# Level products for the later halves, one predicated copy a half, and two modulation steps a part: a decoder kernel of two blocks on Trainium2

## The reference

```python
b = jnp.cumsum(gt, axis=2)                      # gt: log of the forget gate
diff = b[:, :, :, None, :] - b[:, :, None, :, :]
decay = jnp.exp(jnp.where(causal, diff, -jnp.inf))
attn = jnp.einsum('bhtd,bhsd,bhtsd->bhts', qt, kt, decay)
o = einsum('bhts,bhsv->bhtv', attn, vt) + einsum('bhtd,bhdv->bhtv', qt * exp(b), state)
state = exp(b_last) * state + einsum('bhsd,bhsv->bhdv', kt * exp(b_last - b), vt)
```

## Time and profile before

| | |
|---|---|
| runs | 2058.63 us median of 3 (2056.67 to 2058.8) |
| profiled execution | 2055.89 us, span of its instructions 2054.0 us |
| PE busy | 1671.7 us (81%) |
| DVE busy | 1047.3 us (51%) |
| POOL busy | 668.8 us (33%) |
| ACT busy | 550.0 us (27%) |
| DMA | 309 GB/s mean over the span |
| mean granted TensorE clock | 0.924 |

### The profile page before, as it was taken

The page is one execution under the profiler, slowest core; times in us unless marked ns, Lnnn a source line. Parts: engine busy times, 40 slices in busy tenths (PEclk is TensorE's granted clock), DMA queues, the critical chain, the costliest instruction groups (busy, mean ns, idle before and its releaser), DMA issues.

```text
span 2054.0 us, 21828 instructions
## 1 busy us (share of the span) xinstructions
PE 1671.7 (81%) x8580; PEld 1024.8 (50%) x8580; DVE 1047.3 (51%) x1910; ACT 550.0 (27%) x948; POOL 668.8 (33%) x413
## 2 busy tenths in 40 slices
PE   6979887787777777787999988999998877677766
PEld 5866852232232223236989868987894221121211
DVE  6955576876778675453664897554434100000001
ACT  4422431122212212124453435445621000000001
POOL 4422553444444444423664555433320000000000
PEclk9999898999999999998999999999998877777777
DMA  8655499999999999974545323544585999999997
GB/s 328 237 200 225 153 376 422 421 421 421 422 422 420 409 422 421 418 328 146 185 144 174 125 102 104 200 164 148 189 349 202 408 421 421 422 421 421 422 421 305
DMA packets 92212, 634.73 MB, mean 309 GB/s; under 512 B 10924, under 2 KB 13612, under 8 KB 16456
## 3 DMA queue, kind: packets, MB, share of 16 engines
q1 hardware_dynamic: 50400, 351.82, 43.7%
q0 software_dynamic: 36864, 268.45, 31.7%
q10 hardware_dynamic: 4840, 13.00, 1.8%
HBM read 632.15 MB, written 1.08 MB: 308 GB/s over the span
## 4 chain that ended last, share of the span: by engine, by line
DMA 40%; PE 36%; DVE 16%; issue 4%; ACT 3%; POOL 0%; ACTq 0%; DVEq 0%; SPq 0%; POOLq 0%
DMA t<-in_expert_uv,t 19%; DMA t<-in_eg 5%; DMA t<-in_ed 5%; DMA ring<-in_ed 5%; PE ps L538 4%; PE ps L540 4%; PE ps L542 4%; PE ps L709 3%; DVE t L1927 3%; PE ps L710 3%; PE ps L585 3%; DVE t L1721 3%; DMA ring<-in_eg 3%; PE ps L572 2%; PE ps L557 2%
## 5 line engine op out<-in xcount | busy, mean ns | idle before, releaser
L168 POOL TENSOR_TENSOR t<-ring,t 128x1024 fp32r<-128x1024 f32 x143 | 370.7, 2601 | 459.1 <-ACT t L160 458.7
L709 PE MATMUL ps<-t 128*128 128x512 f32 x496 | 277.2, 642 | 157.8 <-ACT t L1314 157.7
L2575 POOL DMA_INDIRECT t<-in_expert_uv,t x248 | 284.1, 1146 | 357.2 <-PE ps L710 336.0
L1927 DVE CUSTOM_DVE_ANT_0 t<-t 128x1024 f32<-128x1024 f32 x248 | 302.7, 1225 | 173.6 <-DMA t<-in_expert_uv,t 171.0
L160 ACT ACTIVATE t<-ring 128x1024 fp32r<-128x1024 f32 x220 | 230.0, 1054 | 243.4 <-PE ps L542 92.7
L710 PE MATMUL ps<-t 128*128 128x512 f32 x496 | 262.3, 611 | 0.0
L709 PEld LDWEIGHTS ps<-t 128*128 128x128 f32 x496 | 88.0, 196 | 321.1 <-ACT t L1314 255.2
L999 PE MATMUL ps<-t 128*32 128x512 f32 x864 | 149.1, 787 | 71.6 <-DMA t<-in_ed 25.6
L538 PE MATMUL ps<-t 128*128 128x256 f32 x1120 | 164.6, 290 | 26.1 <-POOL t L168 9.1
L538 PEld LDWEIGHTS ps<-t 128*128 128x128 f32 x1120 | 147.6, 195 | 36.6 <-issue 28.0
L168 DVE TENSOR_TENSOR t<-ring,t 128x1024 fp32r<-128x1024 f32 x77 | 109.7, 1434 | 108.8 <-ACT t L160 108.2
(11 more groups left out here) (349 smaller groups left out, 1947.5 us busy)
## 6 DMA issues: line engine op xcount, KB each, us to landing
ring<-in_w_in SPq DMA_DIRECT2D x82, 1024.0 KB, 4.9
t<-in_eu SPq DMA_DIRECT2D x38, 1024.0 KB, 26.5
t<-in_eg SPq DMA_DIRECT2D x36, 1024.0 KB, 26.9
t<-in_ed SPq DMA_DIRECT2D x34, 1024.0 KB, 27.5
ring<-in_ed SPq DMA_DIRECT2D x30, 1024.0 KB, 27.0
ring<-in_eg SPq DMA_DIRECT2D x28, 1024.0 KB, 27.0
ring<-in_eu SPq DMA_DIRECT2D x26, 1024.0 KB, 27.0
ring<-in_ada_w SPq DMA_DIRECT2D x20, 1024.0 KB, 6.9
```

Source lines behind the costliest of these rows:

```text
L168: e.tensor_tensor(p.lo, p.view, p.hi.bitcast(F32), ALU.subtract).then_inc(self.w.lo[eng], 1)
L709: e.matmul(sums[tt][0], s.diag[col % 4], v[:, 1024:1536], start=first, stop=last)
L1927: ins = e.tensor_tensor_reduce(out=g[:, 0:1024], in0=g[:, 0:1024], in1=s.hN[:, col // 128, :], scale=1.0, scalar=0.0, op0=ALU.mult, op1=AL ...
L2575: m.gathered[s.place[col]].up(e.indirect_dma_start(out=s.gb[col], out_offset=None, in_=m.a_in["expert_uv"], in_offset=bass.IndirectOffsetO ...
```

## The change

In the recurrence, PE multiplies the whole of Gt by only the odd blocks of it (64 of 128 columns), eight products fill one bank with 64 columns each, and DVE copies the bank at once into the odd blocks of `acc` under the odd blocks of the mask. The diagonal stays as it was, under names of its own. The take of a half-level moves behind the next half-level's `scaled` and `decays`, ahead of its `kept`. The rests of the 16 parts of bi and bg are made by DVE instead of POOL.

In the first mixers, every gate part is followed by two modulation steps (before: one in branch 0, two in branch 1), on PE, ACT and DVE alike. The chunks are ordered to match: a modulation pair behind each of the eight `w_in` pairs, `wbp` behind the sixth pair, `wbc` last; `pour(ada, 8)` is gone from the output product. DVE makes the whole convolution before the gates' takes.

```diff
+def odd(t, at, tile, l):
+    dims = [[2 * l, 64 // l]] * (l < 64) + [[1, l]] * (l > 1)
+    return free_dims(t[:, at + l:at + l + 1], [tile, 8], *dims)
+
+def packed(t, l):
+    return free_dims(t[:, 0:1], [64, 8], *([[l, 64 // l]] * (l < 64) + [[1, l]] * (l > 1)))
@@ lay_out @@
-    for n in range(8):
-        if n > 5:
-            s.ada.append(m.w.ada_pair(a["ada_w_2"][n - 1]))
+    for n in range(6):
         s.sp.expect(pair(a["w_in"], n), "G" if n in (0, 4) else "GV", "cols")
-        if n < 5:
-            s.ada.append(m.w.ada_pair(a["ada_w_2"][n]))
-        if n in (5, 7):
-            s.sp.expect(pair(a["wbp" if n == 5 else "wbc"], 0), "GV", "wide")
-    s.ada.append(m.w.ada_pair(a["ada_w_2"][7]))
+        s.ada.append(m.w.ada_pair(a["ada_w_2"][n]))
+    s.sp.expect(pair(a["wbp"], 0), "GV", "wide")
+    for n in range(6, 8):
+        s.sp.expect(pair(a["w_in"], n), "GV", "cols")
+        s.ada.append(m.w.ada_pair(a["ada_w_2"][n]))
+    s.sp.expect(pair(a["wbc"], 0), "GV", "wide")
...
-    t_("GV", 9, 10, 7, 8), n_("G", 11, 12, 13, 14), t_("G", 29, 30)
+    t_("GV", 9, 10, 7, 8), n_("V", 11, 12, 13, 14), t_("G", 29, 30)
@@ gate parts in pe_mixers1, act_mixers1, dve_mixers1 @@
-                pour(ada, 1 + br)
+                pour(ada)
@@ before or between the output products, on all three @@
-    pour(ada, 8)
@@ pe_recurrence (diagonal(hf) keeps the old products, key ("lv", "diag", q)) @@
+    def products(lv, hf):
+        l = 1 << lv
+        ps = b.claim(e, ("lv", lv, hf))
+        for j in range(8):
+            at = hf * 1024 + j * 128
+            later = h.Gt[:, at:at + 128].rearrange("p (b two t) -> p b two t", two=2, t=l)[:, :, 1, :]
+            ins = e.matmul(ps[:, j * 64:j * 64 + 64], h.Gt[:, at:at + 128], later, start=True, stop=True)
+        b.told(ins, ("lv", lv, hf))
@@ dve_mixers1: the body of convolved() runs at once, before the loop over br @@
-            if br == 0:
-                pour(conv, 1)
@@ dve_recurrence (kept_diagonal(hf) keeps the old copies) @@
+    def kept(lv, hf):
+        key, l = ("lv", lv, hf), 1 << lv
+        e.wait_ge(*b.full(key))
+        for before in ([("lv", lv - 1, hf)] if lv else [("lv", "diag", 2 * hf), ("lv", "diag", 2 * hf + 1)]):
+            e.wait_ge(*b.taken(before))
+        b.emptied(e.copy_predicated(odd(h.acc, hf * 1024, 128, l), odd(h.masks, lv * 128, 0, l),
+                                    packed(b.ap(key), l)), key)
...
-            kept(lv - 1 if lv else 7, done[lv + 1], done[lv], hf)
-            takes(e, s.sp, 1)
+            if lv or hf:
+                takes(e, s.sp, 1)
+            if lv:
+                kept(lv - 1, hf)
+            else:
+                kept_diagonal(hf)
+    takes(e, s.sp, 1)
     for hf in range(2):
-        kept(6, 6, 5, hf)
+        kept(6, hf)
```

More of the change, by code:

```diff
@@ L842, in pe_recurrence, with diagonal @@
     filler = filling()
-    def products(lv, hf, lhs, rhs):
+    def diagonal(hf):
         for q in range(2 * hf, 2 * hf + 2):
-            ps = b.claim(e, ("lv", lv, q))
+            ps = b.claim(e, ("lv", "diag", q))
             for j in range(4):
@@ L849, in products @@
                 sl = slice(half * 128, half * 128 + 128)
-                ins = e.matmul(ps[:, j * 128:j * 128 + 128], b3(lhs)[:, hd, sl], b3(rhs)[:, hd, sl],
+                ins = e.matmul(ps[:, j * 128:j * 128 + 128], b3(h.bk)[:, hd, sl], b3(h.bq)[:, hd, sl],
                                start=True, stop=True)
-            b.told(ins, ("lv", lv, q))
+            b.told(ins, ("lv", "diag", q))
+    def products(lv, hf):
[6 more added lines that the diff above has]
+        b.told(ins, ("lv", lv, hf))
     e.wait_ge(*m.forget.turn("pe", 2))
@@ L856, in pe_recurrence @@
     for hf in range(2):
-        products("diag", hf, h.bk, h.bq)
+        diagonal(hf)
     for lv in range(7):
@@ L860, in pe_recurrence @@
             e.wait_ge(*m.factors.turn("pe"))
-            products(lv, hf, h.Gt, h.Gt)
+            products(lv, hf)
             pour(filler, 1)
@@ L871, in pe_recurrence @@
         b.told(ins, ("cross", q))
-    e.wait_ge(*b.taken(("lv", 6, 3)))
+    e.wait_ge(*b.taken(("lv", 6, 1)))
     e.wait_ge(*b.taken(("bi", 1, 1)))
@@ L1277, in act_mixers1 @@
         act_norm(m, e, m.x, s.pf_f, (tt,))
-        if tt == 0:
-            pour(ada, 8)
         if tt == 0:
@@ L1767, in dve_mixers1 @@
     e.wait_ge(*b.taken(("v", 1)))
[L1769 to L1782, removed]
+    m.v(e.tensor_tensor(s.cu[:, :, 2:258], s.cu[:, :, 2:258], s.zv, ALU.mult))
+    for g in range(4):
+        m.v(e.tensor_scalar(s.cy[:, g, :], s.cu[:, g, 0:256], s.cvw[:, g:g + 1], None, ALU.mult))
+        for k in (1, 2):
+            m.v(e.scalar_tensor_tensor(out=s.cy[:, g, :], in0=s.cu[:, g, k:k + 256],
+                                       scalar=s.cvw[:, 4 * k + g:4 * k + g + 1], in1=s.cy[:, g, :],
+                                       op0=ALU.mult, op1=ALU.add))
+    m.conv_y.up(e.tensor_tensor(s.cy, s.cy, s.zb, ALU.mult))
     for br in range(2):
@@ L2154, in scaled @@
         if lv:
-            e.wait_ge(*b.full(("lv", lv - 1, 2 * hf + 1)))
+            e.wait_ge(*b.full(("lv", lv - 1, hf)))
         e.tensor_tensor(Ge, Ee, ke, ALU.mult)
@@ L2159, in dve_recurrence, with kept_diagonal @@
     e.wait_ge(m.d_hgrn.sem, 32)
-    def kept(mask, lv, before, hf):
+    def kept_diagonal(hf):
         for q in range(2 * hf, 2 * hf + 2):
-            e.wait_ge(*b.full(("lv", lv, q)))
-            if before is not None:
-                e.wait_ge(*b.taken(("lv", before, q)))
+            e.wait_ge(*b.full(("lv", "diag", q)))
             b.emptied(e.copy_predicated(
-                acc3[:, 4 * q:4 * q + 4, :], free_dims(h.masks[:, mask * 128:mask * 128 + 128], [0, 4], [1, 128]),
-                r3(b.ap(("lv", lv, q)), 4)), ("lv", lv, q))
+                acc3[:, 4 * q:4 * q + 4, :], free_dims(h.masks[:, 896:1024], [0, 4], [1, 128]),
+                r3(b.ap(("lv", "diag", q)), 4)), ("lv", "diag", q))
+    def kept(lv, hf):
[5 more added lines that the diff above has]
+                                    packed(b.ap(key), l)), key)
     e.wait_ge(m.forget.sem, 2)
@@ L2173, in dve_recurrence @@
     e.wait_ge(*b.taken(("bq", 1, 1)))
-    done = [None, "diag", 0, 1, 2, 3, 4, 5, 6]
     for lv in range(7):
```

## The result

The changed kernel took 2039.52 us median of 4 runs (2036.84 to 2041.26), the kernel before 2058.72 of 4 (2056.67 to 2060.21) beside it: ratio 0.9906, interval [0.9889, 0.9923], 19.2 us faster. Forecast were 2037.6 and a range of 2028 to 2047. The profiled execution took 2036.84 us (span 2035.0), that of before 2055.89; forecast was 2034.9.

A forecast was written before the change was run, and what follows sets the result against it. In the recurrence DVE stalls beside POOL's rests and PE waits; in the first mixers PE waits for rests and late weights. -14.8 - 6.2 = -21.0 us: 2034.9 from the profiled execution, 2037.6 from the median; range 2028 to 2047.

The forecast's parts named there:

- Recurrence, forecast -14.8: Recurrence: 0.5 us gained on entry and 14.3 in the level loop; bounds -9.9 and -16.9.
- The loop: Level loop of the recurrence: 13 half-levels fall from 5.62 to 4.52 us each, 14.3 gained.
- DVE 4.36, so PE with 4.52 becomes the bound: Recurrence half-level: DVE's work sums to 4.36 us, PE's products and filler to 4.52, so PE binds.
- the copy: Recurrence: DVE's one strided predicated copy of 512 elements takes 0.63 us, as each old one did.
- third rival: Strided access slows the recurrence's copies; at 1.9 us each the half-level is the old 5.62; chance 0.08.
- The entry: Before the level loop: three rests join DVE's queue behind the second scan, first L2156 at about 1154.0, 0.5 us gained.
- the columns moved: First rival, recurrence: columns set the products' time, DVE binds at 4.36, 2.1 us more gained, 2035.5; chance 0.12.
- First mixers, forecast -6.2: First mixers: 4.3 us gained up to the output product, 1.9 within it; bounds nothing and -11.
- the wait of 8.9: First mixers: PE idles 9.2 us before part 21 behind DVE's convolution, then a cold part of 5.25 at 1.2 GHz.
- one sum ... is gone from there: -1.9: First mixers: one modulation sum between the halves of the output product goes, saving 1.9 us.
- the likeliest case: Whole kernel: the forecast itself, chance 0.56, with its own range 2032 to 2042.
- The second rival: First mixers gain nothing through PE's long wait and lower clock; 6.2 us less gained, 2043.8; chance 0.24.

The follow-up runs named there:

- experiment 6: Changed kernel with the predicated copy writing its elements side by side instead of at strided places (output not the reference's): 2038.27 or 2038.29 us, one run.
- Experiment 3: Changed kernel with the rests of bi and bg made by POOL again instead of DVE: 2044.68 us, one run.
- experiment 4: Changed kernel with products of 128 columns into two banks a half and two predicated copies, rests still on DVE: 2046.98 us, one run.
- experiment 9: The changed kernel again, unchanged: 2040.35 us, ratio 0.9902 to the kernel before.
- experiment 8: Changed kernel with POOL waiting for the last gating before it makes the first low parts of w_q: 2036.56 us, ratio 0.9879 to the kernel before.
- experiment 7: Changed kernel with the first mixer's convolution made two steps at a time during the first branch's product: 2031.22 us, ratio 0.9866 to the kernel before.
- experiments 7 and 10: Experiment 7, and the changed kernel with both the late convolution and POOL's wait before w_q's low parts: 2027.82 us, ratio 0.9834 to the kernel before.
- experiment 2: Kernel before with only the first mixers of the change: 2054.58 us, ratio 0.9982 [0.9971, 0.9992].

## Why the prediction was right, and where its sizes were off

**Recurrence, forecast -14.8, alone -14.7.** The sum came out right because two errors of 1 us cancel, which is luck; and the interval of 9 to 16 us would have passed other sums too. The loop was to gain 14.3 and gained 13.2 (5.62 to 4.61). The step "DVE 4.36, so PE with 4.52 becomes the bound" holds for ten of the thirteen half-levels. The term that was mis-sized is the copy: taken at 0.63 from start to start at every level, it took 1.12 so measured (1.32 in its own record) at l = 1 and 2, because of the destination's steps (experiment 6); the other 0.4 us of the loop are half-levels of 4.55 where PE was taken at 4.52. I had argued from L2156 and its like, which step through SBUF too; they don't show what the predicated copy costs. By the third rival's own account 1.9 would have undone the gain; this costs 0.7.

The entry was to gain 0.5 and gained about 1.5. I added three rests to DVE's queue behind a scan that I took at its 4.5. But the scan was itself standing still for POOL's rest, like L2143; it takes 2.28 alone. Of these 2.2 only 1.0 came through: the first pair of `decays` ended by 1144.4, but ACT had its table only at 1145.6, a load that the forecast left out. The Trainium skill ("DVE: opcode table, instruction layouts, handler registers and perf-mode slots", Datapath and trigger behaviour) says that the built-in scan runs at half throughput. Twice the 1.22 of a subtraction of 1024 elements gives 2.4 as an estimate by that page; the 2.28 agree, and 4.5 would have looked too long by it. The Trainium skill ("SBUF — State Buffer", Who interferes with whom) says that a DVE instruction with two SBUF inputs contends with a GpSimd instruction that reads SBUF, over a shared read interface. Experiment 3 agrees: both scans and L2149 are long when POOL has the rests, by 2.2 and 2.0 us, beside a POOL operation of 2.5.

That the columns moved don't set the product's time is shown by experiment 4 (4.52 with 128, 4.55 with 64).

**First mixers, forecast -6.2, alone -4.0.** The part up to the output product was forecast at 78.1 and took 78.89 and 78.94 (experiment 9): the wait of 8.9, its cause and the cold start came as said, the wait because the start and the length of the convolution, 2.2 off each, cancel, and the cold part a little shorter (4.84 instead of 5.25). Against them stand 1.4 us more of waiting for the last gating. The step that failed is "one sum ... is gone from there: -1.9". It is gone, but the output product's stretch didn't get shorter. I had followed the freed loads only as far as the gates' weights, not to what stands behind them in the order: w_q now lands early, POOL splits it beside the last gating, PE waits 1.4 longer, and its next 56 matmuls take 1.7 longer at the lower clock. With POOL held back alone, the output product up to its last eight matmuls takes 25.01 against 27.11 before (26.70 in the changed kernel): the term as forecast. The rest of what was missing is the gap ahead of part 40: 3.6 before, 4.5 and 4.3 in the changed kernel's two traces, 4.8 in experiment 8, 3.9 and 4.0 in experiments 7 and 10. Where the profile puts it down to POOL, the operation that it names (207.84, 2.34 us in the changed kernel) is the rest of part 43; those of parts 40 to 42 were done by 171.29, and in experiments 7 and 10 PE starts before that operation ends. So it isn't POOL's rest that PE waits for there; what it is, no run shows.

**Range and chances.** The outcome lay 1.9 above the forecast, within the likeliest case's own range. The second rival (the first mixers gain nothing, 2043.8) falls with experiment 2, whose interval ends below 1, though a third of their gain was missing for a reason like the one it named.

## What to carry to other kernels

When an engine's operation is to be costed, look whether the row at hand was itself stalled: on DVE every form with two SBUF inputs that is longer than its like, scans too, may be waiting for POOL. Even the scaling of one tile by a number can: L1734, 0.48 alone, took 2.62 beside a rest of POOL's in experiment 7. Where loads are freed, follow them to the first one that isn't wanted yet, and ask what its splitting will collide with; here one wait on POOL gave 3 us back. And work that is due later should not be put ahead of an engine's only supplier: the convolution before the gates cost 7 to 8 us of TensorE's time, and during the branch product little.

## What the runs showed of the hardware that was not expected

A predicated copy of 512 elements from PSUM takes 0.72 us when it writes runs of four or more fp32 columns, or all side by side, and 1.32 when it writes single columns or pairs with as wide a gap between them. Strides in the mask cost nothing, and an ordinary product of two tiles that writes in the same steps takes 0.73 at most. A scan over 1024 fp32 elements takes 2.28 us, and 4.50 beside a POOL subtraction that reads SBUF, both in the changed kernel's own trace.
